# A gated delta recurrence in token layout with streaming state, and pairs at a seam between two blocks

## The reference, cut to what matters

```python
def step(S, xs):
    q_c, k_c, u_c, w_c, qk_c, gl_c = xs
    v_new = u_c - jnp.einsum('bhcd,bhde->bhce', w_c, S)
    o_c = jnp.einsum('bhcd,bhde->bhce', q_c, S) + jnp.einsum('bhcs,bhse->bhce', qk_c, v_new)
    S = S * jnp.exp(gl_c)[..., None, None] + jnp.einsum('bhcd,bhce->bhde', k_c, v_new)
    return S, o_c
...
o = jnp.swapaxes(o_fwd + o_bwd, 1, 2)
o = _rmsnorm(o, head_norm_w) * jax.nn.silu(z.reshape(B, T, H, Dh))
```

## Time and profile before

| | us |
|---|---|
| median of 3 runs | 2192.77 |
| lowest and highest | 2188.11, 2194.53 |
| the profiled execution | 2192.9 |
| its span | 2191.1 |

### The profile page before, as it was taken

The page is one execution under the profiler, slowest core; times in us unless marked ns, Lnnn a source line. Parts: engine busy times, 40 slices in busy tenths (PEclk is TensorE's granted clock), DMA queues, the critical chain, the costliest instruction groups (busy, mean ns, idle before and its releaser), DMA issues. The chain is left out here.

```text
span 2191.1 us, 23767 instructions
## 1 busy us (share of the span) xinstructions
PE 1662.4 (76%) x9150; PEld 805.6 (37%) x9150; DVE 738.6 (34%) x1678; ACT 441.9 (20%) x949; POOL 327.7 (15%) x317
## 2 busy tenths in 40 slices
PE   6998879979887877879888676666666666667665
PEld 6987855545333333349676411111111011111110
DVE  3256266776767767544652200000000000000001
ACT  4256133223213212135310200000000000000001
POOL 0042023433433333310230000000000000000000
PEclk9999989999889989989896788777777777777777
DMA  6451469999999999965002599999999999999997
GB/s 238 135 173 59 144 279 382 420 420 421 419 421 421 421 421 421 421 273 205 1 2 116 226 420 420 420 420 420 421 421 420 421 421 421 420 421 421 420 420 322
DMA packets 111666, 738.56 MB, mean 337 GB/s; under 512 B 14048, under 2 KB 15712, under 8 KB 27616
## 3 DMA queue, kind: packets, MB, share of 16 engines
q1 hardware_dynamic: 74432, 468.91, 52.9%
q0 software_dynamic: 36864, 268.45, 29.6%
q10 hardware_dynamic: 288, 0.08, 0.0%
HBM read 736.35 MB, written 1.05 MB: 337 GB/s over the span
## 5 line engine op out<-in xcount | busy, mean ns | idle before, releaser
L2406 PE MATMUL ps<-arena,xe 128*32 128x512 f32 x2048 | 377.7, 829 | 202.1 <-DMA arena<-in_experts_in 200.5
L1093 PE MATMUL ps<-arena 128*128 128x512 f32 x820 | 409.7, 651 | 115.3 <-ACT arena L1275 109.7
L2477 DVE TENSOR_TENSOR low<-low,ps 128x512 f32<-128x512 f32 x16 | 11.0, 688 | 889.6 <-PE ps L2406 889.6
L1093 PEld LDWEIGHTS ps<-arena 128*128 128x128 f32 x820 | 165.4, 208 | 341.1 <-issue 198.9
L1481 DVE CUSTOM_DVE_ANT_0 arena<-arena,ps 128x1024 f32<-128x1024 f32 x205 | 247.8, 1219 | 126.1 <-DMA arena<-in_peer,arena 126.0
L988 POOL DMA_INDIRECT arena<-in_peer,arena x205 | 196.9, 961 | 435.7 <-PE ps L1093 332.6
L2406 PEld LDWEIGHTS ps<-arena,xe 128*32 128x32 f32 x2048 | 48.6, 123 | 520.1 <-DMA arena<-in_experts_in 497.6
L2430 PE MATMUL ps<-arena,hT 128*32 128x512 f32 x1024 | 165.4, 750 | 77.2 <-DMA arena<-in_experts_down 65.4
L2506 POOL TENSOR_TENSOR low<-h,hT 128x512 f32<-128x512 f32 x2 | 2.5, 1265 | 944.9 <-DVE h L2490 944.9
L1275 ACT ACTIVATE arena<-ident,arena 128x128 f32<-128x128 f32 x256 | 83.5, 391 | 149.0 <-DVE arena L1491 146.2
L2430 PEld LDWEIGHTS ps<-arena,hT 128*32 128x32 f32 x1024 | 26.2, 122 | 198.7 <-DMA arena<-in_experts_down 160.8
(11 more groups left out here) (424 smaller groups left out, 1944.4 us busy)
## 6 DMA issues: line engine op xcount, KB each, us to landing
arena<-in_experts_in SPq DMA_DIRECT2D x256, 1024.0 KB, 26.9
arena<-in_experts_down SPq DMA_DIRECT2D x128, 1024.0 KB, 27.1
ring<-in_stream SPq DMA_DIRECT2D x44, 512.0 KB, 4.5
arena<-in_stream SPq DMA_DIRECT2D x36, 512.0 KB, 4.3
arena<-in_stream SPq DMA_DIRECT2D x14, 1024.0 KB, 6.9
arena<-in_peer,arena POOLq DMA_INDIRECT x205, 18.3
h<-in_x SPq DMA_DIRECT2D x1, 1024.0 KB, 5.8
arena<-in_sel SPq DMA_DIRECT2D x1, 1024.0 KB, 5.7
```

The source lines that it names most:

```text
L1093: last = nc.tensor.matmul(ps[:, 4 + 2 * t + half, :], diag[:, n % DIAGS, :], slot(n)[:, D + half * BANK:D + (half + 1) * BANK], start=firs ...
L2406: last = nc.tensor.matmul(ps[32 * j:32 * (j + 1), 4 + r // KB, :], xe[:, k, :], w[:, j * BANK:(j + 1) * BANK], start=(k == 0), stop=(k == ...
```

## The change

The recurrence computes its outputs token by token: `qdec` and `qkm` are now stationary (64 columns), the state and `vnew` stream (128 columns), and the result has tokens on the partitions. TensorE takes one direction after the other instead of interleaving them. There is a state buffer for each step and there are two buffers for `vnew` (in the space of `kb_` and `vb`), so the update no longer waits for outputs; the outputs of direction 1 of a step come after the `wT` products of the next step. ScalarE evacuates the first four output halves, VectorE adds the other four to them directly from PSUM. The norm runs along the free axis: ScalarE squares and sums block 1, VectorE block 0, VectorE scales, TensorE transposes, VectorE multiplies by the head's gain and the gate. An activation with root stands ahead of the recurrence on ScalarE.

At the seam, quads 61 and 62 go in pairs, and the low parts of units 0 and 1 are made by VectorE, unit 0 between the scaling and the evacuation, unit 1 after the activations' low parts.

```diff
-        size = 2 if j < HALVED else 1 if j == QUADS - 1 else G
+        size = 2 if j < HALVED or QUADS - 3 <= j < QUADS - 1 else 1 if j == QUADS - 1 else G
...
-            for u in range(2):
-                pool.wait_ge(f_high, u + 1)
-                high, low = parts_of(u)
-                nc.gpsimd.tensor_tensor(low, raw2(u), high.bitcast(F32), ALU.subtract).then_inc(f_low0, 1)
...
-                if u < 2:
-                    pe.wait_ge(f_low0, u + 1)
-                else:
-                    pe.wait_ge(f_low, u - 1)
+                pe.wait_ge(f_low, u + 1)
...
             second_scale(1)
+            mix2_low(0)
             second_evacuate(1)
             second_low(1)
-            for u in range(2, F_UNITS):
+            for u in range(1, F_UNITS):
                 mix2_low(u)
...
+    by_side = lambda x: x.rearrange("p (d q) c -> p d q c", d=2)
+    vnew = [tok2[:, 0, :, :, :], by_side(kb_[:, 8:16, :])]
+    state = [None, tok2[:, 1, :, :, :], by_side(vb[:, 0:8, :]), by_side(vb[:, 8:16, :])]
...
+            def outputs(st, d):
+                c, u0, cols, t, half = place(st, d)
+                n = 2 * st + d
+                if 2 <= n < 6:
+                    pe.wait_ge(o_sb, n - 1)
+                elif n >= 6:
+                    pe.wait_ge(o_sum, n - 5)
+                for q in range(4):
+                    dst = ps[cols, 4 + d, q * P:(q + 1) * P]
+                    if st:
+                        nc.tensor.matmul(dst, qdec[:, u0 + q, cols], state[st][:, d, q, :], start=True, stop=False)
+                    last = nc.tensor.matmul(dst, qkm[cols, d, t, q, :], vnew[st % 2][cols, d, q, :], start=(st == 0), stop=True)
+                last.then_inc(o_ps, 1)
+
             for st in range(4):
                 if st:
+                    for d in range(2):
+                        c, u0, cols, t, half = place(st, d)
+                        pe.wait_ge(s_sb, 2 * (st - 1) + d + 1)
+                        for q in range(4):
+                            last = nc.tensor.matmul(ps[cols, 2 + d, q * P:(q + 1) * P], wT[:, u0 + q, cols], state[st][:, d, q, :],
+                                                    start=True, stop=True)
+                        last.then_inc(v_ps, 1)
+                    outputs(st - 1, 1)
+                for d in range(2 if st < 3 else 0):
+                    c, u0, cols, t, half = place(st, d)
+                    pe.wait_ge(v_sb, 2 * st + d + 1)
                     for q in range(4):
+                        last = nc.tensor.matmul(ps[:, 6 + d, q * P:(q + 1) * P], kdec[cols, u0 + q, :], vnew[st % 2][cols, d, q, :],
+                                                start=True, stop=True)
+                    last.then_inc(s_ps, 1)
+                pe.wait_ge(v_sb, 2 * st + 1)
+                outputs(st, 0)
+            pe.wait_ge(v_sb, 8)
+            outputs(3, 1)
+
+            for n, t in enumerate((1, 0)):
+                pe.wait_ge(on_r, n + 1)
+                for hd in range(DHEADS):
+                    last = nc.tensor.transpose(ps[:, t, hd * P:(hd + 1) * P], od[:, 0, t, hd, :], ident[:, :])
+                last.then_inc(on_ps, 1)
...
+            def add_sides(st, d):
+                c, u0, cols, t, half = place(st, d)
+                dve.wait_ge(o_ps, 2 * st + d + 1)
+                dve.wait_ge(o_sb, 4)
+                nc.vector.tensor_tensor(od[cols, 0, t, :, :], od[cols, 1 - d, t, :, :], bank4(4 + d)[cols], ALU.add).then_inc(o_sum, 1)
...
-                        dve.wait_ge(o_ps, n + 1)
                         for q in range(4):
-                            last = nc.vector.scalar_tensor_tensor(state[:, d, q, :], state[:, d, q, :], egl[:, t, d, half, q:q + 1],
-                                                                  bank4(6 + d)[:, q, :], ALU.mult, ALU.add)
+                            last = nc.vector.scalar_tensor_tensor(state[st + 1][:, d, q, :], state[st][:, d, q, :],
+                                                                  egl[:, t, d, half, q:q + 1], bank4(6 + d)[:, q, :], ALU.mult, ALU.add)
...
+            add_sides(3, 0)
+            add_sides(3, 1)
+            dve.wait_ge(o_sum, 4)
+            link(nc.vector.tensor_tensor(od[:, 1, 0, :, :], od[:, 0, 0, :, :], od[:, 0, 0, :, :], ALU.mult))
+            link(nc.vector.reduce_sum(orn[:, 0, :], od[:, 1, 0, :, :], AX.X))
+            dve.wait_ge(on_sq, 1)
+            nc.vector.tensor_scalar(orn[:, :, :], orn[:, :, :], 1.0 / DK, EPS, ALU.mult, ALU.add).then_inc(on_ms, 1)
             dve.wait_ge(on_rt, 1)
+            link(nc.vector.reciprocal(orn[:, :, :], orn[:, :, :]))
+            for t in (1, 0):
+                nc.vector.tensor_tensor(od[:, 0, t, :, :], od[:, 0, t, :, :], orn[:, t, :].unsqueeze(2).broadcast_to([P, DHEADS, P]),
+                                        ALU.mult).then_inc(on_r, 1)
+            for n, t in enumerate((1, 0)):
+                dve.wait_ge(on_ps, n + 1)
+                cols = slice(t * P, (t + 1) * P)
+                nc.vector.scalar_tensor_tensor(oT[:, 0:4, cols], bank4(t), head_norm[:, 0:1], z[:, :, cols], ALU.mult, ALU.mult).then_inc(o_ready, 1)
...
+            nc.scalar.activation(warm[:, :], ones[:, 0:1], ACT.Sqrt)
+            for n, (st, d) in enumerate(steps[:4]):
                 c, u0, cols, t, half = place(st, d)
                 act.wait_ge(o_ps, n + 1)
+                nc.scalar.activation(od[cols, d, t, :, :], bank4(4 + d)[cols], ACT.Copy).then_inc(o_sb, 1)
+            act.wait_ge(o_sum, 3)
+            for hd in range(DHEADS):
+                last = nc.scalar.activation(od[:, 1, 1, hd, :], od[:, 0, 1, hd, :], ACT.Square, accum_out=orn[:, 1, hd:hd + 1])
+            last.then_inc(on_sq, 1)
```

82 lines of the change are left out of this document (16 added, 66 removed).

## The result

The changed kernel took 2171.24 us (median of 5, 2167.48 to 2177.3) against 2192.77 us before (by now the median of 5 runs, 2188.11 to 2196.17): ratio 0.9912, 95% interval 0.9896 to 0.9928. The forecast was 2174.9 us, range 2166 to 2186. The profiled execution has a span of 2169.4 us against 2191.1.

A forecast was written before the change was run, and what follows sets the result against it. The end was taken as bound by the expert-weight DMA stream, whose start waits for TensorE. Gains of 7.6 (recurrence), 6.9 (norm) and 3.5 (seam) sum to 18.0 us: 2192.9 - 18.0 = 2174.9, range 2166 to 2186.

The forecast's parts named there:

- Rival 5: Whole kernel: the change does not reach the end, the expert stream's start being held elsewhere; 2193 us, 3%.
- rival 2: Recurrence: clock low; 24.0 us more over the whole and 1 in the transposes, 2199.9, 6%; half of it 2187, 7%.
- half of the stretch: Recurrence: the clock is low for half of it; 2187 us, 7%.
- Rival 1: Recurrence: changes of tile shape are nearly free, so it ends at 23.6 us; 2167.2 us in all, 15%.
- rival 4: Recurrence: weight loads and streams run in turn, adding 14.1 us; 2189 us, 4%.
- 208 x 0.11 + 53 x 0.145: Recurrence, TensorE: 208 records at 0.11 us, 22.9, plus about 53 changes of tile shape at 0.145, 7.7 us.
- the 7.6 us: Recurrence: forecast gain, 31.3 us at full clock against 38.9 before.
- Norm: From the last outputs to the output projection: 6.4 us in place of 13.3, a gain of 6.9 us.
- no change: Output projection: starts cold at clock 0.50 as before, no change, give or take 1.5 us.
- Seam: Between the blocks: pairs and low parts on VectorE gain 3.5 us, from both sides 1 and 4.2.
- ScalarE is late next: Seam: VectorE would be 4.2 us earlier, but ScalarE then limits, with the root at 969.1 in place of 972.61.
- Rival 3: Seam: it brings nothing, as three engines interlock there; 2178.4 us, 10%.

The follow-up runs named there:

- e8: Changed kernel with the low parts of units 0 and 1 back on GpSimd, pairs kept; single execution, 2178.8 us.
- e6: Changed kernel with each output batch ordered by shape, all four state products then all four chunk products (result incomplete); 2164.84 us, ratio 0.9869.
- e4: Changed kernel with both output batches right behind kdec and the state update waiting for them; 2177.69 us, ratio 0.9948.
- e5: Kernel before, old order, with spare matmuls in the recurrence's waits including seven in its first gap; 2187.48 us, ratio 0.9984.
- e10: e7 with odd and even steps' outputs in different banks, later additions, seven spare matmuls in the first gap, bank opened once; 2161.55 us, ratio 0.9853.
- e1: Kernel before with only the two seam edits (quads 61 and 62 in pairs, low parts on VectorE); 2192.16 us, ratio 0.9992.
- e2: Kernel before with only the new recurrence and norm; 2173.41 us, ratio 0.9913.
- e9: Changed kernel with outputs by shape as in e6, but only the first head opening the bank's accumulation, keeping the whole sum; 2167.21 us, ratio 0.9884.
- e7: e6 with both directions' outputs interleaved in two column halves, state products before kdec, chunk products after; 2165.78 us, ratio 0.9876.
- e3: Kernel before, old order, with spare matmuls in the recurrence's waits, its first gap not filled; 2188.8 us, ratio 0.9996.
- e12: Changed kernel with quads 61 and 62 whole again, low parts kept on VectorE; single execution, 2176.59 us.
- e11: Changed kernel with seven spare matmuls in the recurrence's first gap; 2170.8 us, ratio 0.9899.

## Why the prediction was right, point by point

**The bound.** That the end follows the start of the expert stream was right: the first expert matmul came 22.5 us earlier (1230.66 for 1253.21) and the span ended 21.7 us earlier. Rival 5 is out.

**Clock.** Full clock in the whole new recurrence, as taken: 1.00 in the window, TensorE busy 98%. Neither case of rival 2 occurred in this profile, and that was in part luck: its mechanism exists all the same, and nothing in the forecast tells the executions with the fall from those without. It was seen in e8: with the same recurrence, 6.8 us at half clock made it 32.6 us in place of 29.4. The forecast priced half of the stretch at 12 us and gave it 7%; what occurs is a fifth of it for 3 us. The changed kernel's own runs spread over 9.8 us.

**Records and shapes.** 0.11 us a record: 8 records in 1.08 us (1128.05 L2120), (1.08 - 0.27) / 7 = 0.116. 0.145 a change of shape: 0.36 for two records and a change leaves 0.14 (0.13 with 0.116), and 0.151 by e6. Rival 1 is out. By the Trainium skill ("TensorE: Matmul & The Clock Gate", Part 3) a load overlaps only another row group's matmul. That would give rival 4's 2189; the rows after disagree with it as those before did, with 0.11 us for 128-column records in one row group.

**The mis-sized term.** The recurrence was forecast at 31.3 us and took 28.7 to the last addition. The step that was off is the count "208 x 0.11 + 53 x 0.145", which lets every record follow the one before. TensorE's busy time, 28.11, is 2.5 us under its 30.6. Where one direction's batch follows the other's in the other half of the array (of the columns for v, of the rows for kdec), records of both run at once: a v batch of 16 and the change behind it take 1.52 us from start to start (1129.06 to 1130.58) and kdec's 1.61 and 1.64 (1126.44 to 1128.05, 1131.59 to 1133.23), not 16 x 0.11 + 0.145 = 1.9. Three of each make 3 x 0.38 + 3 x 0.28 = 2.0 us; the rest is at the borders of v and outputs (1136.12 to 1137.26). The prediction said "two matmuls no longer lie in two halves of the array at once", which is right inside a batch and wrong at its edge. No experiment took just this overlap away; it is read from starts.

**Why faster at all.** The prediction named the streaming state, and e4 shows it: 6.3 us more without it, though some 3 of them are its half clock. But it gave as the reason for the 7.6 us that the state update no longer waits, and set 31.3 us at full clock against 38.9 of which 26.9 were at half clock, without pricing the clock apart. By e5 and the steps of the kernel before the clock is nearly all of it, about 8.5 of the 9.5 us; at equal clock the new order is worth about 1 us. By e6 and e10 its 53 changes of shape and its outputs one direction at a time take back most of what the streaming gives: e10, which keeps the streaming and takes these two out, is some 11 us below the old order at full clock (19.1 against 30.4). The size was right, and the reason named for it only in small part.

**Norm.** 6.4 forecast, 6.6 measured; the projection behind it began at clock 0.50 as before (3.85 us; 4.15 before), "no change" as taken.

**Seam.** 3.5 forecast, 3.9 measured, and L1093's (now L1088's) end 4.2 us behind the last dot, forecast 4.0. "ScalarE is late next" was right, by a hair: from its two splits at 962.31 on ScalarE is never idle until the root at 967.67, which follows its table load (966.37 + 1.28 = 967.65), and VectorE's small sums had ended at 967.54 (967.38 + 0.16). The root comes 8.0 us behind the start of the last dot, forecast 8.4 (969.1 - 960.71); that is the 0.4 by which the seam beat its forecast. The split of the gain, by marks: pairs 2.1 us (picks' end 6.3 to 4.2 behind the dot), low parts 1.8 (10.4 to 8.6 behind it). By variants the split is not the same: e8, with the pairs alone, has 15.85 us, 0.9 less than before, because with them both products meet GpSimd. Rival 3, that the seam brings nothing, was right about e1's time and wrong about its cause.

**What else moved.** 1.0 us at the front, 0.6 between, -0.9 behind: single executions differ by this much, as e2 shows, and nothing of it is explained here.

## What to carry to other kernels

Count TensorE's fp32 work in three terms: records, changes of tile shape, and which neighbours lie in different halves of the array; the second is removed for nothing by reordering (e9), the third is used by interleaving (e7, e10), if the bank is opened once and the next batch has a bank of its own. When a serial stretch is shortened, read its pieces at fixed marks in both traces: e1 has a ratio of 0.9992, and its profiled execution shows 4.3 us gained and 5.5 lost to the clock. And before a gain is put down to a new order, price the old order at the clock of the new one, from its own steps at either clock: here 9.9 and 14.55 us for the same step.

## What the runs showed of the hardware

- A change of tile shape (128 rows by 64 columns to 64 by 64, fp32) costs 0.15 us at full clock: 36 fewer gave 5.45 us.
- The same recurrence step (old order, with 64-column and 128-column records and its waits) took 9.9 us at a granted clock of 1.00 and 14.55 at 0.50.
- Behind one and the same wait the granted clock falls or holds, and these runs do not show what decides it. The first gap of the recurrence is 1.34 us of idle time in the new order and 1.79 to 1.80 in the old. In e1, e3, e7 and e8 the clock fell to 0.50 within 0.1 to 0.4 us of the first kdec behind it; in the kernel before (where it fell 12 us later), the changed kernel, e2, e4, e6, e9 and e12 it stayed at 1.00. With seven spare matmuls in the gap (e5, e10, e11) it stayed in all three; since it also stayed in seven of eleven without, that the filling does it is not shown. In e3, e7 and e8 it came back after about 7 us, in e1 not before the end of the recurrence (44.45 us at 0.51).
- The clock also fell with hardly a gap: in e5 at 1160.0, when TensorE had been busy 29.30 of the 31.22 us before.
- Records in opposite column halves need not start in the order of the program: in the changed kernel outputs (L2119) start at 1137.10, ahead of the last records of the v product (L2129, 1137.20 and 1137.31) that stands before them; in e10 outputs (L2123) start at 1131.48 and v records (L2139) that stand before them at 1131.59.
- Interleaved fp32 outputs in two column halves: 16 records in 1.09 us, where one half at a time needs 1.9 (e7); 8 records in one half with the change behind them take 1.01 us (e6).
- A GpSimd subtraction of 128x1024 fp32 beside a VectorE product of 128x512 stretches the latter from 0.69 to between 2.1 and 2.6 us, each of the three times that they meet (before, and twice in e8). Twice the product ends 0.54 to 0.56 us after GpSimd's last subtraction (969.56 and 969.02 before, 969.80 and 969.24 in e8), as if it had waited for it and then run. The addition that takes one input from PSUM (L1595) took 0.67 us beside the same subtraction (966.96 in e8).
